# Three-block transformer stack: first two weight chunks and the first x, split in pieces

## The reference, cut to what matters

```
def rmsnorm(x, g):
    y = xf * lax.rsqrt(jnp.mean(xf * xf, axis=-1, keepdims=True) + NORM_EPS)
    return (y * g).astype(x.dtype)
hn = rmsnorm(h, norm_g[i])
q, k, v, z = split_proj(hn, w_in_a[j], N_KV_A)      # proj = h @ w_in, 1024 x 2304 for the first layer
q, k = apply_rope(q, cos, sin), apply_rope(k, cos, sin)
```

## Time and profile before

| | |
|---|---|
| median of 3 runs | 871.32 us (870.62 to 871.99) |
| the profiled execution's own time | 871.46 us |
| its span | 869.6 us, 12040 instructions |
| TensorE busy | 855.7 us (98%) |
| VectorE busy | 564.7 us (65%) |
| ScalarE busy | 503.1 us (58%) |
| GpSimd busy | 122.6 us (14%) |
| loads | 146.14 MB, mean 168 GB/s |

### The profile page before, as it was taken

The page is one execution under the profiler, slowest core; times in us unless marked ns, Lnnn a source line. Parts: engine busy times, 40 slices in busy tenths (PEclk is TensorE's granted clock), DMA queues, the critical chain, the costliest instruction groups (busy, mean ns, idle before and its releaser), DMA issues.

```text
span 869.6 us, 12040 instructions
## 1 busy us (share of the span) xinstructions
PE 855.7 (98%) x4414; PEld 700.7 (81%) x4414; DVE 564.7 (65%) x999; ACT 503.1 (58%) x899; POOL 122.6 (14%) x99
## 2 busy tenths in 40 slices
PE   8999999999999999999999999999999999999996
PEld 5877888778888878888888888888878888888885
DVE  6966866777776878755555446576888655555444
ACT  6668466765877764644444334777764644444332
POOL 0121053110153420000000000153320000000000
PEclk9999999999999999999999999999999999999999
DMA  9823564355444336655565555444336655665531
GB/s 312 279 64 104 189 197 140 102 190 173 155 137 145 110 133 209 209 181 179 190 194 193 194 192 171 150 144 145 100 143 194 210 181 191 193 193 179 191 116 48
DMA packets 94765, 146.14 MB, mean 168 GB/s; under 512 B 6516, under 2 KB 54900, under 8 KB 94708
## 3 DMA queue, kind: packets, MB, share of 16 engines
q1 hardware_dynamic: 92820, 139.52, 49.3%
q0 software_dynamic: 1296, 4.72, 1.7%
q10 hardware_dynamic: 592, 1.14, 0.4%
HBM read 144.32 MB, written 1.05 MB: 167 GB/s over the span
## 4 chain that ended last, share of the span: by engine, by line
PE 92%; DVE 4%; issue 2%; ACT 2%; DMA 1%; SPq 0%; POOLq 0%; POOL 0%; DVEq 0%; ACTq 0%
PE bank L1176 78%; PE bank L1124 7%; PE bank L1325 2%; PE bank L1253 1%; PE bank L1231 1%; PE bank L1228 1%; DVE lo L1023 1%; DMA raw<-in_w_in_a 1%; PE bank L1256 1%; DVE hyb_acc L1982 1%; ACT hyb_MT L1567 0%; PE bank L1332 0%; ACT L1567 0%; DVE bank L1889 0%; ACT hi L1346 0%
## 5 line engine op out<-in xcount | busy, mean ns | idle before, releaser
L1023 DVE TENSOR_TENSOR lo<-raw,hi 128x1024 fp32r<-128x1024 f32 (+1 forms) x244 | 297.4, 1248 | 101.3 <-ACT hi L1346 98.4
L1346 ACT ACTIVATE hi<-raw 128x1024 fp32r<-128x1024 f32 (+1 forms) x260 | 266.8, 1058 | 107.4 <-PE bank L1176 104.2
L1176 PE MATMUL bank<-hi,xT_hi 128*128 128x512 f32 (+2 forms) x736 | 289.7, 394 | 0.3 <-DVE lo L1675 0.2
L1176 PE MATMUL bank<-hi,xT_lo 128*128 128x512 f32 (+2 forms) x736 | 282.6, 384 | 0.0
L1176 PE MATMUL bank<-lo,xT_hi 128*128 128x512 f32 (+2 forms) x736 | 281.8, 383 | 0.0
L1176 PEld LDWEIGHTS bank<-hi,xT_hi 128*128 128x128 f32 x736 | 138.3, 188 | 30.3 <-issue 4.3
L1176 PEld LDWEIGHTS bank<-hi,xT_lo 128*128 128x128 f32 x736 | 138.2, 188 | 28.1
L1176 PEld LDWEIGHTS bank<-lo,xT_hi 128*128 128x128 f32 x736 | 138.6, 188 | 24.7
L1176 PE MATMUL bank<-hi,hT 128*128 128x512 f32 x352 | 109.5, 390 | 0.0
L1176 PEld LDWEIGHTS bank<-hi,hT 128*128 128x128 f32 x352 | 66.1, 188 | 13.7
L1176 PE MATMUL bank<-hi,oT_hi 128*128 128x512 f32 x160 | 66.4, 415 | 2.2 <-DVE lo L1023 2.2
(11 more groups left out here) (252 smaller groups left out, 926.5 us busy)
## 6 DMA issues: line engine op xcount, KB each, us to landing
raw<-in_w_in SPq DMA_DIRECT2D x26, 1024.0 KB, 5.1
raw<-in_w_gate SPq DMA_DIRECT2D x44, 512.0 KB, 4.0
raw<-in_w_up SPq DMA_DIRECT2D x44, 512.0 KB, 5.0
raw<-in_w_down SPq DMA_DIRECT2D x22, 1024.0 KB, 4.9
raw<-in_w_out SPq DMA_DIRECT2D x20, 1024.0 KB, 5.0
raw<-in_w_in_b SPq DMA_DIRECT2D x10, 1024.0 KB, 5.1
raw<-in_w_in_a SPq DMA_DIRECT2D x7, 1024.0 KB, 7.1
raw<-in_w_in_a SPq DMA_DIRECT2D x4, 256.0 KB, 5.4
```

Of the source, the lines that this page charges most:

```text
L1023: return engine.tensor_tensor(lo[r][:, cols], raw[c.i % RAW][:, cols], hi[r][:, cols].bitcast(F32), ALU.subtract)
L1176: last = nc.tensor.matmul(bank[:, 0:wd], still[a], mv[r][:, off:off + wd], start=c.first and i == 0 and j == 0, stop=c.last and i == len(t ...
L1346: nc.scalar.activation(hi[c.i % SPLIT][:, cols], raw[c.i % RAW][:, cols], ACT.Copy)\
```

## The change

Both chunks 0 and 1 are loaded, rounded and subtracted in four pieces of one row tile. TensorE does both row blocks of x for each piece before it goes to the next; of chunk 0 it does k = 0, 1, 2 at "chunk 0" and k = 3 at "rest 0", behind the turning of the second half of x. x is turned two tiles at a time into a bank (`x_rows`); ScalarE rounds it out of PSUM with the gain column as its scale, VectorE makes the low part out of PSUM with the same column in one fused operation (`x_split`), and `first_x` is gone. All four squares come after "rest 0", with the mean and the Newton step. The identity is loaded by ScalarE's queue, the gain rows by GpSimd's. A ScalarE copy of one column stands at its start. The dummy matmuls read one column repeated, and are 7 at the start and 1 at "begin"; the 3 behind the first turn are gone.

```diff
-def first_turn(sc, n, m):
+def x_rows(sc, n, m, q):
 
     b = sc.bank()
-    s = sc.step("first_turn", n=n, m=m, bank=b)
-    b.freed = (s, "vector")
-    return s
-
-
-def first_split(sc, of):
-
-    sc.turned[of.n, of.m] = sc.step("first_split", of=of, n=of.n, m=of.m)
+    return sc.step("x_rows", n=n, m=m, q=q, bank=b)
+
+
+def x_split(sc, rows):
+
+    n, m, q = rows.n, rows.m, rows.q
+    s = sc.step("x_split", n=n, m=m, q=q, of=rows, bank=rows.bank)
+    rows.bank.freed = (s, "vector")
+    sc.split_x[n, m, q] = sc.turned[n, m] = s
...
-    first = first_turn(sc, 0, 0)
-    sc.step("piece")
-    first_split(sc, first)
-    sc.step("piece")
-    first = first_turn(sc, 0, 1)
-    sc.step("piece")
-    sc.step("piece")
-    first_split(sc, first)
+    rows = {(m, q): x_rows(sc, 0, m, q) for m in range(M) for q in range(2)}
+    for q in range(2):
+        for m in range(M):
+            x_split(sc, rows[m, q])
+            sc.step("piece")
     sc.step("begin")
 
     def second():
-        first = [first_turn(sc, 1, m) for m in range(M)]
-        sc.step("second_weights")
-        first_split(sc, first[0])
-        sc.step("second_weights")
-        first_split(sc, first[1])
-        squares(sc, 0)
-
-    sc.soon += [second, lambda: (squares(sc, 1), factor(sc, "h"))]
+        rows = {(m, q): x_rows(sc, 1, m, q) for m in range(M) for q in range(2)}
+        sc.step("piece")
+        sc.step("piece")
+        for q in range(2):
+            for m in range(M):
+                x_split(sc, rows[m, q])
+        sc.step("piece")
+        sc.step("piece")
+
+    sc.soon += [second, lambda: (squares(sc, 0), squares(sc, 1), factor(sc, "h"))]
...
-    if s.kind == "second_weights":
-        return [(1, s.i)]
...
-    warm, _ = at("warm", [P, 512], BF16, place[0] - 2 * 12 * S * 4)
+    warm, _ = at("warm", [P, 1], BF16, place[0] - 2 * 12 * S * 4)
     gain_rows8, _ = at("gain_rows8", [KD, P], F32, place[0] - 2 * 12 * S * 4 + 1024)
     gain_cols, _ = at("gain_cols", [P, KD], F32, place[0] - 2 * 12 * S * 4 + 1536)
-    first_x = [at(f"first_x{i}", [P, 512], F32, place[0] - 2 * 12 * S * 4 + 2048 * (i + 1))[0] for i in range(4)]
...
-        total[c.i % RAW] += 16 * len(c.loads)
+        total[c.i % RAW] += 16 * len(c.loads) if c.i >= 2 else 0
...
-            def first_rows(m):
-                sp.dma_start(h[:, m, 0:512], x[:, m, 0:512]).then_inc(x_first[m], 16)
-
-            first_rows(0)
-            sp.dma_start(cst[:, 0:P], t["cst"][:, 0:P]).then_inc(const_in, 16)
+            sp.dma_start(h[:, 0, 0:512], x[:, 0, 0:512]).then_inc(x_first[0], 16)
...
-                if c.i == 0:
+                if c.i < 2:
 
                     _, (wt, c0, cw, ks) = c.loads[0]
-                    for k in ks:
-                        sp.dma_start(slot[:, k * cw:(k + 1) * cw], wt[:, k, c0:c0 + cw])\
-                          .then_inc(raw_first[k] if k < 3 else raw_in[0], 16)
+                    for n, k in enumerate(ks):
+                        sp.dma_start(slot[:, n * cw:(n + 1) * cw], wt[:, k, c0:c0 + cw])\
+                          .then_inc(piece_in[k], 16)
                         if k == 0:
-                            first_rows(1)
-                    return
-                if c.i == 1:
-
-                    _, (wt, c0, cw, ks) = c.loads[0]
-                    for half, done in enumerate((second_in, raw_in[1])):
-                        k0 = ks[0] + 2 * half
-                        sp.dma_start(slot[:, 2 * half * cw:2 * (half + 1) * cw].rearrange("p (k n) -> p k n", n=cw),
-                                     wt[:, k0:k0 + 2, c0:c0 + cw]).then_inc(done, 16)
+                            sp.dma_start(h[:, 1, 0:512], x[:, 1, 0:512]).then_inc(x_first[1], 16)
                     return
...
-                nc.tensor.matmul(psum[3][:, :], warm[:, 0:P], warm[:, :], start=True, stop=True)
+                nc.tensor.matmul(psum[3][:, :], spread(warm[:, :], [P, P]), spread(warm[:, :], [P, 512]),
+                                 start=True, stop=True)
 
         pe.wait_ge(warm_up, 1)
-        warmed(6)
+        warmed(7)
...
-            if s.kind == "first_turn":
+            if s.kind == "x_rows":
                 pe.wait_ge(x_in if s.n else x_first[s.m], 16)
                 bank = freed(pe, s.bank)
-                for i in range(4):
-                    c0 = s.n * 512 + i * P
+                for i in range(2):
+                    c0 = s.n * 512 + (2 * s.q + i) * P
                     last = transpose(bank[:, i * P:(i + 1) * P], h[:, s.m, c0:c0 + P])
-                last.then_inc(sem["first_turn", "tensor"], 1)
-                if s.i == 0:
-                    warmed(3)
+                last.then_inc(sem["x_rows", "tensor"], 1)
             if s.kind == "begin":
-                warmed(3)
+                warmed(1)
+            if s.kind in ("chunk", "rest") and s.i < 2:
+
+                c, half = (s, 0) if s.kind == "chunk" else (s.of, 1)
+                for k in ((0, 1, 2), (3,))[half] if c.i == 0 else ((0, 1), (2, 3))[half]:
+                    if k % 2 == 0:
+                        pe.wait_ge(piece_lo, (4 * c.i + k) // 2 + 1)
+                    else:
+                        split_done(pe, c.i, k // 2)
+                    for b, wd, ts, m in c.outs:
+                        ended(pe, sc.split_x[c.i, m, k // 2], "vector")
+                        _, kt, off = ts[k]
+                        still = [x[:, kt, m * P:(m + 1) * P] for x in xT]
+                        for j, (a, mv) in enumerate(((0, hi), (0, lo), (1, hi))):
+                            last = nc.tensor.matmul(
+                                psum[2 * b["pair"] + m][:, 0:wd], still[a], mv[c.i][:, off:off + wd],
+                                start=c.first and k == 0 and j == 0, stop=c.last and k == 3 and j == 2)
+                        if c.last and k == 3 and m == 0:
+                            last.then_inc(part_done, 1)
+                if half:
+                    last.then_inc(sem["chunk", "tensor"], 1)
+                continue
...
-                if half == 0 and c.i:
+                if half == 0:
...
-                        if half == 0 and n == 0:
-                            if c.i == 0 and i % 2 == 0:
-                                pe.wait_ge(first_lo, i // 2 + 1)
-                            elif c.i == 0:
-                                split_done(pe, c.i, i // 2)
-                            elif 2 * i == len(ts):
-                                split_done(pe, c.i, 1)
+                        if half == 0 and n == 0 and 2 * i == len(ts):
+                            split_done(pe, c.i, 1)
...
-            if c.i == 1 and half == 0:
-                act.wait_ge(second_in, 16)
-            elif half == 0 or c.i == 1:
+            if half == 0:
...
         def piece(k):
-            cw = chunks[0].size // 4
-            cols = slice(k * cw, (k + 1) * cw)
-            act.wait_ge(raw_first[k] if k < 3 else raw_in[0], 16)
-            nc.scalar.activation(hi[0][:, cols], raw[0][:, cols], ACT.Copy)\
-              .then_inc(sem["chunk", "scalar"] if k % 2 else first_hi, 1)
+            c, cw = k // 4, chunks[0].size // 4
+            cols = slice(k % 4 * cw, (k % 4 + 1) * cw)
+            act.wait_ge(piece_in[k], 16)
+            nc.scalar.activation(hi[c][:, cols], raw[c][:, cols], ACT.Copy)\
+              .then_inc(sem["chunk", "scalar"] if k % 2 else piece_hi, 1)
...
-        act.dma_start(gain_rows8[:, :], t["norm_g"][0].rearrange("(k p) -> k p", p=P)).then_inc(columns_in, 16)
+        act.dma_start(cst[:, 0:P], t["cst"][:, 0:P]).then_inc(const_in, 16)
+        act.wait_ge(warm_up, 1)
+        nc.scalar.activation(junk[:, 0:1], warm[:, :], ACT.Copy)
...
-            elif s.kind == "first_split":
-                ended(act, s.of, "vector")
-                done(nc.scalar.activation(xT[0][:, 4 * s.n:4 * s.n + 4, s.m * P:(s.m + 1) * P],
-                                          first_x[s.of.i][:, :].rearrange("p (k t) -> p k t", k=4), ACT.Copy), s)
+            elif s.kind == "x_split":
+                if s.i == 0:
+                    act.wait_ge(sem["columns", "vector"], 1)
+                ended(act, s.of, "tensor")
+                for i in range(2):
+                    k = 4 * s.n + 2 * s.q + i
+                    last = nc.scalar.activation(xT[0][:, k, s.m * P:(s.m + 1) * P],
+                                                psum[4 + s.bank.at][:, i * P:(i + 1) * P], ACT.Copy,
+                                                scale=gain_cols[:, k:k + 1])
+                done(last, s)
...
+        pool.dma_start(gain_rows8[:, :], t["norm_g"][0].rearrange("(k p) -> k p", p=P)).then_inc(columns_in, 16)
         nc.gpsimd.memset(power[:, :], -0.5).then_inc(chain["gpsimd"], 1)
...
         def piece(k):
-            cw = chunks[0].size // 4
-            cols = slice(k * cw, (k + 1) * cw)
-            dve.wait_ge(sem["chunk", "scalar"] if k % 2 else first_hi, k // 2 + 1)
```

(37 more changed lines are left out.)

## The result

The changed kernel takes 873.11 us (median of 22 runs, 872.14 to 874.43), the kernel before 871.4 us (22 runs, 870.62 to 872.11). The ratio is 1.0019, with a 95% interval of 1.0013 to 1.0025: slower by 1.7 us, where 0.8 was forecast. The changed kernel's profiled execution took 873.75 us (span 871.8), 2.29 more than that of before.

What follows compares the result with a forecast made beforehand. TensorE, 98% busy, was taken as the bound. 1.2 us won in front and 0.3 us spare become a 2 us wait in chunk 2: +0.8 us, 872.2 us; own range 871.6 to 872.9, 8 in 10 from 870.4 to 874.2.

Steps and rivals of the forecast that it cites:

- the signs that it named for being wrong: Changed profile: short or missing chunk 2 wait, matmuls 0.44 us apart for microseconds after 8 us, chunk 2 landing before 15.5.
- The mechanism: Chunk 2: four squares and the factor delay its second low half to 23.5 us; TensorE, asking at 21.5, waits 2 us.
- 18 matmuls end at 12.15: TensorE's start: the first 18 real matmuls run without gaps, done at 12.15 us; x's second half is turned by 13.05.
- low-clock rival: Start: fewer fillers leave the first 12 matmuls 0.44 us apart; low half at 25.4, +2.7 us, 874.1; chance 0.20.
- Gain rows landing at 3.5 to 4: Start: the 4 KB load by GpSimd's queue lands at 3.5 to 4 us, within bounds of 3.3 and 7.1.
- Landings: First loads: x's second rows taken to land at 7.0 us, chunk 2, issued at about 5.9, at 16.2.
- Moving 64 KB to another queue frees no engine: First loads: DMA engines already 0.95 busy from 3 to 7 us, so the identity's new queue leaves chunk 2's landing unchanged.
- The second rival: Faster transfers in the first loads: everything lands 1.3 us sooner, chunk 2 at 14.9; -0.5 us, 870.8; chance 0.12.
- First real matmul at 7.95: TensorE's start: x's second rows at 7.0 us, then four transposes (0.66) and one dummy lead to 7.95.
- Prices of single steps: Start: dummies 0.44 us each, ending near 4.0; x parts 0.25 on ScalarE; fused operations on VectorE between 0.2 and 0.5.
- Chunk 2 at 20.05: TensorE begins chunk 2 at 20.05 us, 1.2 us earlier than 21.26, and asks for its second half at 21.5.
- the 1.2 us won in front: TensorE's gain before chunk 2 from the earlier, gapless start; forecast to turn into a wait inside chunk 2.

Runs made afterwards that it cites:

- Experiment 1: Changed kernel with squares and norm's factor one entry later, behind both low halves of chunk 2: 871.23 us, ratio 1.0 to the kernel before.
- experiment 2: Kernel before with its first two squares moved behind "rest 0", nothing else changed: 872.34 us, ratio 1.0013.
- experiment 3: Changed kernel with more dummy matmuls: 9 at the start, 3 behind the first turn, 2 at "begin": 871.91 us, ratio 1.0009 to the kernel before.
- Experiment 4: Changed kernel with the gain rows loaded by ScalarE's queue ahead of the identity: 872.46 us, ratio 1.0013 to the kernel before.
- experiment 10: Changed kernel, squares and factor later but ahead of chunk 3's rounding, gain rows by ScalarE's queue, 7, 3 and 2 dummies: 869.77 us, ratio 0.9987.
- 8: Kernel before with only the mean of squares and Newton step one entry later: 871.24 us, ratio 0.9998.
- experiment 11: Kernel before without the three dummies behind the first turn and with one at "begin" instead of three: 871.48 us, ratio 1.0002.
- 5: Changed kernel, squares and factor one entry later, gain rows by ScalarE's queue, 7, 3 and 2 dummies: 871.15 us, ratio 0.9996 to the kernel before.
- 6: Changed kernel, squares and factor one entry later, 9, 3 and 2 dummies, gain rows still by GpSimd's queue: 870.32 us, ratio 0.9987.
- Experiment 7: Kernel before with only the queues changed, identity by ScalarE's and gain rows by GpSimd's: 871.3 us, ratio 0.9998.
- 9: Changed kernel, squares and factor later but ahead of chunk 3's rounding, 9, 3 and 2 dummies, gain rows by GpSimd's queue: 870.15 us, ratio 0.9989.

## Why the prediction was right and its size was not

The 873.11 us lie in the prediction's wide range (870.4 to 874.2) and just outside the forecast's own (871.6 to 872.9). Two of the signs that it named for being wrong came: matmuls after 8 us stood 0.43 apart for 3.6 us, and chunk 2 landed before 15.5, at 15.2. The third, a short or missing wait, did not: the wait was there, 1.60 us. So the mechanism was found, and the time fell into the wide range by the help of a rival that the prediction held for less likely.

- **The mechanism: right.** All four squares follow the rounding of chunk 2's first half, the factor holds the low half, TensorE stands still inside chunk 2. Experiment 1 takes it away and the loss is gone; experiment 2 puts the later squares alone into the kernel before and makes it slower. From the rounding to the last read-out 4.17 us were measured (17.55 to 21.72), 4.08 forecast; from there to TensorE's going on 3.24, forecast 3.15.
- **The mis-sized term: "18 matmuls end at 12.15", and so the start of ScalarE's chain.** They ended at 14.07, since nine took 0.43 us. The x parts began at 14.49, not 12.5, and the rounding at 17.55, not 16.3; 0.7 of the 2.0 us went into the time that the forecast had ScalarE wait for chunk 2. The 1.25 us that are left, with the 0.2 of the two spans above, are the step from 23.5 to 24.96. The prediction had this as its low-clock rival (25.4 and 874.1) and called it the less likely; the profiled execution is that rival, with nine slow matmuls instead of twelve. In experiment 3 the pace is the high one and 1.0 of after's 1.7 us is back, with the overlap of intervals said there.
- **Gain rows landing at 3.5 to 4: mis-sized.** 4 KB by GpSimd's queue, issued at 1.26, took 3.7 us and landed at 4.9, inside the bounds. TensorE idled 0.96 us for it ahead of the real stream. Experiment 4 takes that idling away; its median is 0.5 us nearer to before, which the intervals do not tell from nothing.
- **Landings: wrong, without effect in after.** "Moving 64 KB to another queue frees no engine" failed: x's second rows came at 5.4 and not 7.0, chunk 2 at 15.2 and not 16.2, though it was issued at 6.3 and not 5.9 (with two entries more and one fewer ahead of it, it could hardly be earlier than the 6.03 of before). Chunk 2 then lay 2.3 us unread, since ScalarE was the late one. The second rival's landing nearly came true (14.9), but its gain did not.
- **First real matmul at 7.95: right (8.02), for another reason.** x's rows came early, the gain rows late and the transposes ran slowly.
- **Prices of single steps: right.** The dummies end at 4.10 (forecast 4.0). x parts on ScalarE are 0.26 us apart (14.49 to 15.26 for three; forecast 0.25); VectorE's fused ones take 0.27 (2.16 for eight).
- **Chunk 2 at 20.05: wrong** (21.77), the mis-sized term again. So the 1.2 us won in front are not there in after's profiled execution, where the slow matmuls took them; in experiment 1 the lead is 0.65 us.

What stays open: how much of after's 1.7 us the clock takes in a typical execution, since only one was profiled; what keeps the high level; and whether the late row behind 160 us takes the 0.65 us of experiment 1.

## What to carry to other kernels

When work moves later on one engine, follow its last result through the next engine's order: a row that nobody needs yet (here the norm's factor) can stand in front of one that TensorE needs now. A faster front pays only if what it meets next is ready; otherwise it becomes a longer wait at the same place. And a dummy matmul that only fills time may be what keeps the next microseconds at full pace: before leaving it out, count what slow matmuls would cost. Here the evidence for it is experiment 3 alone; experiment 4 had the full pace without it and experiment 10 did not have it throughout in spite of three.

## What the runs showed of the hardware

**The rate of the first loads went with the queues that issue them.** From 3 to 7 us the profiled executions, one of each kernel, moved: 269, 255, 268 and 252 GB/s with the identity on SyncE's queue (before, experiments 2, 8, 11); 302, 303 and 296 with gain rows and identity both on ScalarE's (4, 5, 10); 366, 356, 359, 338, 366 and 371 with the identity on ScalarE's and the gain rows on GpSimd's (after, 1, 3, 6, 7, 9). The busy share of the DMA engines was 0.86 to 0.95, 0.98 to 1.01 and 1.02 to 1.05: it rises far less than the rate. Over the longer window from 1 to 8 us the means are 229 to 240, 268 to 270 and 270 to 291 GB/s: the step that stays clear is the one that comes with the identity leaving SyncE's queue. The Trainium skill (Trainium Kernel Development and Optimization, Key Constraints) says that several issuers share the same engines and save issue time alone; the rate here does not follow that, and the measurement decides. Why the rate differs is open.

**The lower clock at the start lasts differently long from run to run.** Ends of the stretch at 0.43 us a matmul: 12.0 us in after, 9.5 in experiment 1, 10.3 in experiment 10; no such stretch among the real matmuls of experiments 3, 4, 6 and 9. What TensorE did before differs: it idled 0.96, 1.09 and 1.01 us ahead of its first transpose in after, 1 and 10, and 0, 0.28, 0 and 0.80 in 3, 4, 6 and 9. Experiment 7 idled 1.01 us there too, and its real matmuls were at the high pace (eleven from 9.65 to 12.19); 2 and 8 idled 1.56 and 1.03 us a little later, ahead of their second transposes, and were at the high pace as well. So no idle stretch explains the slow starts alone, and what decides them stays open. The runs of after spread over 2.3 us, those of experiment 3, with fillers, over 0.6; that the clock makes this spread was not shown. The granted clock showed it in experiment 11 (0.59) and not in after (1.00 between 8 and 12 us): in such a case the distance from one matmul to the next says more than the record. The Trainium skill (TensorE: Matmul & The Clock Gate, Part 1: The HAM clock gate) says that one kernel shows different counts of slow matmuls at its start from run to run; after and experiment 1, nine and three of them with the same program up to there, agree.
